# Output weights' low parts over the raw ones, the router's turned x in the queries' buffer, three buffers handed to expert weights earlier

## The chip, the cores and the metric

The kernel runs on one core of a Trainium2 chip. The metric is device time in microseconds (us) for one execution. All weights lie in the chip's main memory (DRAM) and are read during the run. The core's five engines run side by side: PE (matmuls), DVE and ACT (elementwise work, copies out of the accumulator memory), POOL (here small loads and a few elementwise operations) and SP, which in this kernel does nothing but issue transfers, in a fixed order, and wait for the semaphores ahead of each.

## The reference, cut to what matters

Two transformer blocks in float32 over 256 positions of width 1024. The first block ends in a mixture of 32 experts, of which each position uses two; the kernel reads the weights of all 32.

```python
y = concat([swa_sink_mixer(h_a), dilated_mixer(h_b), mla_mixer(h_c)]) @ w_out   # 1024 x 1024
x = layer_norm(ALPHA * x + y, ln1_g, ln1_b)
g_logits = x @ w_rg + b_rg                    # router: 4 groups, then 8 experts of the group
...
def block_ffn(xb, e):
    return (silu(xb @ w_gate[e]) * (xb @ w_up[e])) @ w_down[e]     # 3 MB of weights for each e
...
x = layer_norm(ALPHA * x + y_moe, ln2_g, ln2_b)
# then two layers: x = x + rms_norm(mixers(rms_norm(x) @ w_in[l]) @ w_out[l], post_norm[l])
```

## The kernel before

**Stages.** First the input products and the attention of the first block ("tile1" and "bv" jobs make queries, keys and values; steps A, C and B are the heads of its three mixers), then the output product ("y1"), layer norm and router ("logit", "rank"), then the experts, then the two layers of the second block.

**Split products.** The large products are made in three passes of a fast float format: a weight is split into a high part (ACT, line 1664, `high`) and a low part, weight minus high part (DVE, line 2336, `low`). The activations are split likewise into `a_high`, and `x_low` or `mix_low`. A split is a piece of weights for one product. The high parts lie in `w_high`, the low ones in `w_low`, each of six units of 4 KB per partition. `y1` has four splits, `w_out0` to `w_out3`, each of two units. Semaphore `lows` counts low parts done, `p_ready` counts products of PE done.

**Memory.** The buffer `ring` has 12 slots of 1 MB. The buffers of the split products lie over it: `w_high` is slots 5, 6, 7, `w_low` is slots 8, 9, 10, `a_high` is slot 11, `x_low` is the buffer `xT` and `mix_low` is `mixT` (the block at line 439 allocates them and frees them, so that `ring`, `xT` and `mixT` come to lie on the same addresses). Slots 0 to 4 take raw weights of the mixers in turn. After the last input product nothing reads `x_low`; ACT then writes the turned x for the router there (job `x1t`, line 1504), and PE reads it (line 1073).

**Expert weights.** Four experts form a bunch, so there are 8 bunches of 12 MB, each of 12 items of 1 MB: items 0 to 3 hold rows 0 to 511 of gate and up of the four experts, items 4 to 7 rows 512 to 1023, items 8 to 11 the down weights. Counted through, item n is item n mod 12 of bunch n div 12. On PE a bunch is `gate_up(b, 0)`, `gate_up(b, 1)` (line 1324), the gather of the rows of the next bunch (line 1280), `down(b)` (line 1339) and the sum into the output (line 1307). The semaphore `gu_half` is raised after the first, `gu_ready` after the second, `y_ready` twice in `down`.

**Who waits for what.** `load_expert` issues one item after `free_for_experts` has waited until its buffer is free. The first 21 items go to 21 buffers in the order of `FIRST_LOADS` (line 133): the 12 slots, and nine buffers of the attention stage that are free by then (`K_C`, `TILES_MID`, `BIAS_HIGH`, `BIAS_LOW`, `PROBS_T`, `V_TOP`, `MIX_T`, `LN_ROWS`, `X_T`). Four of them (`ONCE`) are used once, the other 17 in rotation: `expert_slots` (line 144) gives each later item the buffer that was given longest ago. The wait is then on the earlier item's product (`expert_done`: `gu_half` for items 0 to 3 of a bunch, `gu_ready` for 4 to 7, `y_ready` for 8 to 11). In the last bunch the rotation is broken: its items 0 to 3 must go to slots 0 to 3, which the next layers' weights take over (`NEXT_LAYERS`), and slots 9 to 11 are not used (`MORE_SLOTS`, kept for a second round of experts that these inputs do not need). SP issues strictly in program order, so an item whose buffer is not free holds all behind it.

In the kernel before, the bunch before the last has its items 0 to 11 in slots 3, 4, K_C, PROBS_T, V_TOP, 1, 2, 0, 6, 9, 7, 10.

Of the kernel before, what the change touches and what calls it, by code (L numbers as in the profile page):

```python
# [7 lines left out]
F32 = mybir.dt.float32  # L8
# [7 lines left out]
P = 128  # L16
# [107 lines left out]
for _l in range(LAYERS):  # L124
# [7 lines left out]
EARLY = ((0, 3), (1, 4))  # L132
FIRST_LOADS = EARLY + ((2, K_C), (16, TILES_MID), (17, BIAS_HIGH), (18, BIAS_LOW), (3, PROBS_T), (4, V_TOP), (5, 1),
                       (6, 2), (7, 0), (8, 6), (9, 9), (10, 7), (11, 10), (12, 5), (13, 8), (14, 11), (15, MIX_T),
                       (19, LN_ROWS), (20, X_T))
ONCE = (TILES_MID, BIAS_HIGH, BIAS_LOW, LN_ROWS)
# [24 lines left out]
MIXERS_RING = 5  # L161
TWICE_ROUND, LATE_RING = 2 * MIXERS_RING, 3
MEM_AT = 3
PIECES = {f"bunch{b}_{k}": 2 for b in range(BUNCHES) for k in range(GATE_UP)}


def slot_of(n):
    if n < FIRST_EXPERT:
        return n % MIXERS_RING if n < TWICE_ROUND else (n - TWICE_ROUND) % LATE_RING
    return EXPERT_SLOTS[n - FIRST_EXPERT] if n < FIRST2 else (n - FIRST2) % MIXERS_RING  # L170
# [217 lines left out]

LAST_SPLIT = {item_split(n): n for n in range(len(SPLITS))}
OPENING = [SPLIT[("tile1", 0)]] + [SPLIT[("tile2", l, 0)] for l in range(LAYERS)]  # L390
# [36 lines left out]
def build(nc, ins, out):  # L427
    ctx = ExitStack()
    with ctx:
# [8 lines left out]

        with nc.sbuf_tensor("slots_before", [P, MIXERS_RING * SLOT], F32), \
                nc.sbuf_tensor("w_high", [P, UNITS * SLOT // 2], F32R) as w_high, \  # L440
                nc.sbuf_tensor("w_low", [P, UNITS * SLOT // 2], F32R) as w_low, \
                nc.sbuf_tensor("a_high", [P, KC * T], F32R) as a_high, \
                nc.sbuf_tensor("x_low", [P, KC * T], F32R) as x_low, \
                nc.sbuf_tensor("mix_low", [P, KC * T], F32R) as mix_low:
            pass
# [33 lines left out]
        x4 = x_nat[:, :].rearrange("p (t k q) -> p t k q", t=2, k=KC)  # L479
        xT3 = xT[:, :].rearrange("p (k t) -> p k t", k=KC)  # L480
        y_nat = tiles[:, 0:2048].rearrange("p (t d) -> p t d", t=2)
        xT_1 = k_c[:, :].rearrange("p (k t) -> p k t", k=KC)
# [3 lines left out]
        def split_of(n):  # L486

            wide = P if SPLITS[n][0] in OF_TILES else COLS
            a = units_before(n) % UNITS * KC * P
            return [w[:, a:a + KC * wide].rearrange("p (k n) -> p k n", k=KC) for w in (w_high, w_low)]  # L490

# [195 lines left out]
        def _(sp):  # L687
# [53 lines left out]
            def free_for_experts(n):  # L741
# [3 lines left out]
                if earlier:  # L745
                    sp.wait_ge(*expert_done(earlier[-1]))
                elif k < MIXERS_RING:
                    used_up(max(m for m in range(FIRST_EXPERT) if slot_of(m) == k))
                elif k < RING - 1:
                    owners = {UNIT_OWNER[u] for u in range(units_before(OPENING[1])) if u % UNITS // 2 == (k - 5) % 3}  # L750
                    sp.wait_ge(p_ready, max(max(users(n)) for n in owners) + 1)
                elif k == K_C:
                    sp.wait_ge(scores, s_first(STEP[("C", 0, C_HEADS - 1)]) + 1)
                elif k == TILES_MID:
                    sp.wait_ge(scores, s_first(STEP[("B", 0, B_HEADS - 1)]) + 3)
                elif k in (BIAS_LOW, BIAS_HIGH):
                    sp.wait_ge(maxed, STEP[("B", 0, B_HEADS - 1)] + 1)
                elif k in (PROBS_T, V_TOP):
                    sp.wait_ge(o_ready, LAST_OUT_1)
                elif k == LN_ROWS:  # L760
                    sp.wait_ge(ln_done, 2)
                elif k == X_T:
                    sp.wait_ge(p_ready, JOB[("logit", 1)] + 1)
                else:
                    sp.wait_ge(p_ready, JOB[("y1", 3, 1)] + 1)
# [19 lines left out]
            for n in range(FIRST_EXPERT):  # L785
                if n >= MIXERS_RING:
                    used_up(max(m for m in range(n) if slot_of(m) == slot_of(n)))
# [11 lines left out]
                if n == 4:  # L799
                    sp.wait_ge(bias_out, 16)  # L800
                    sp.dma_start(bias3[:, 0:A_HEADS, :], shifted_rows(0, A_HEADS)).then_inc(bias_in, 16)
            for n in [i for i, _ in FIRST_LOADS[len(EARLY):]] + list(range(len(FIRST_LOADS), PER_BUNCH * (BUNCHES - 1))):
                load_expert(FIRST_EXPERT + n)
# [99 lines left out]
        def _(pe):  # L903
# [58 lines left out]
            def run(job, j):  # L962
# [104 lines left out]
                elif kind == "logit":  # L1067
                    tt = job[1]
                    pe.wait_ge(router_scaled, 1)
                    for k in range(KC):  # L1070
                        if k % 4 == 0:
                            from_act(("x1t", tt, k // 4))
                        mm = pe.matmul(dst[:, 0:GROUPS + EXPERTS], xT3[:, k, P * tt:P * tt + P], router[:, k, :],
                                       start=(k == 0), stop=(k == KC - 1))
# [402 lines left out]
        def _(act):  # L1477
# [13 lines left out]
            def take(job, j):  # L1491
# [10 lines left out]
                elif kind == "x1t":  # L1502
                    tt, half = job[1:]
                    op = act.activation(xT3[:, 4 * half:4 * half + 4, P * tt:P * tt + P],
                                        src.rearrange("p (c t) -> p c t", c=4), ACT.Copy)
# [1028 lines left out]
```

## Time and profile before

| | |
|---|---|
| median of 3 runs | 729.3 us (727.13 to 731.64) |
| the profiled execution, its own time | 730.15 us |
| its span | 728.2 us |
| mean granted clock of PE | 0.969 of full speed |
| busy: PE, DVE, ACT, POOL | 661.3, 353.1, 330.1, 43.8 us |
| moved by DMA | 167.84 MB, mean 230 GB/s |

The span is the profiled part of the execution; 1.95 us lie around it. The page cuts the span into 40 slices of 18.2 us and gives for each the busy tenths of each engine and the GB/s moved. Other views give instructions in order of time with the idle time ahead of each and what ended it, sums for chosen stretches, and the chain of work that ended last. A busy PE is not a PE at its peak: matmuls are pipelined and their ends are modelled.

### The profile page before, as it was taken

The page shows a single profiled execution, that of the slowest core. Times are in us where ns is not written, and L with a number is a line of the kernel's source. Part 1 is how long each engine was busy: PE and PEld are TensorE (multiplying, and loading weights), DVE is VectorE, ACT ScalarE, POOL GpSimd, SP SyncE. Part 2 cuts the span into 40 slices and gives each one's busy share as a digit, 9 for nine tenths or more (in the row PEclk, how much of TensorE's full clock was granted, in tenths as well). Part 3 has the DMA queues.
Part 4 walks back from the last instruction along what each step waited for, and adds up shares of the span by engine and source line. Part 5 has one row for each costly group of instructions (what it writes and reads, how often), then busy time and mean ns, then how long its engine had stood idle before and what let it go on. Part 6 is the DMA issues. An engine that isn't in the chain of part 4 may idle for free.

```text
span 728.2 us, 11783 instructions
## 1 busy us (share of the span) xinstructions
PE 661.3 (91%) x4605; PEld 513.0 (70%) x4606; DVE 353.1 (48%) x817; ACT 330.1 (45%) x776; POOL 43.8 (6%) x57
## 2 busy tenths in 40 slices
PE   6989999999899999789796999898979999889986
PEld 5967998789545436335262589877859899778876
DVE  1543656645531021011010557787765487877733
ACT  3465656541011122011120354778864647788642
POOL 6001000000000000000000322000000020100000
PEclk9999999999999999898898999999979999999999
DMA  9995327097999999999999857045533080171301
GB/s 275 338 298 173 118 86 232 23 333 280 363 410 412 412 415 409 415 411 411 416 391 409 268 167 237 1 129 162 161 130 116 15 276 1 57 234 60 114 1 59
DMA packets 94682, 167.84 MB, mean 230 GB/s; under 512 B 4271, under 2 KB 75713, under 8 KB 90529
## 3 DMA queue, kind: packets, MB, share of 16 engines
q1 hardware_dynamic: 92272, 160.88, 61.5%
q0 software_dynamic: 2224, 6.10, 2.5%
q8 instruction: 39, 0.64, 0.4%
q14 instruction: 19, 0.15, 0.1%
q10 hardware_dynamic: 128, 0.08, 0.0%
HBM read 165.96 MB, written 1.07 MB: 229 GB/s over the span
## 4 chain that ended last, share of the span: by engine, by line
PE 58%; SPq 13%; DMA 9%; DVE 8%; ACT 8%; issue 3%; DVEq 0%; ACTq 0%
SPq L777 11%; PE psum L909 11%; PE psum L911 10%; PE psum L910 10%; PE psum L1324 4%; PE psum L1280 3%; DMA values<-in_w_expert_down_dram 3%; PE psum L1214 2%; DMA ring<-in_w_expert_up_dram 2%; PE psum L1339 2%; PE psum L952 2%; PE psum L1044 2%; PE psum L1261 2%; SPq L780 2%; DMA ring<-in_w_in_dram 2%
## 5 line engine op out<-in xcount | busy, mean ns | idle before, releaser
L909 PE MATMUL psum<-a_high,w_high 128*128 128x256 f32 x512 | 150.1, 293 | 8.7 <-DVE w_low L2336 4.6
L911 PE MATMUL psum<-a_high,w_low 128*128 128x256 f32 x512 | 145.4, 284 | 0.0
L910 PE MATMUL psum<-x_low,w_high 128*128 128x256 f32 x512 | 145.3, 284 | 0.0
L2336 DVE TENSOR_TENSOR w_low<-ring,w_high 128x1024 fp32r<-128x1024 f32 (+1 forms) x76 | 107.7, 1429 | 17.4 <-ACT w_high L1664 17.4
L909 PEld LDWEIGHTS psum<-a_high,w_high 128*128 128x128 f32 x512 | 98.6, 193 | 18.5 <-issue 6.8
L1664 ACT ACTIVATE w_high<-ring 128x1024 fp32r<-128x1024 f32 (+1 forms) x79 | 96.1, 1220 | 14.1 <-DMA ring<-in_w_in_dram 10.8
L910 PEld LDWEIGHTS psum<-x_low,w_high 128*128 128x128 f32 x512 | 98.7, 193 | 0.1
L911 PEld LDWEIGHTS psum<-a_high,w_low 128*128 128x128 f32 x512 | 98.6, 193 | 0.0
L1324 PE MATMUL psum<-ring,q_c 128*32 128x512 f32 x336 | 64.6, 708 | 13.5 <-DMA ring<-in_w_expert_up_dram 8.0
L909 PE MATMUL psum<-w_high,a_high 128*128 128x256 f32 x240 | 69.9, 291 | 0.1
L910 PE MATMUL psum<-w_low,a_high 128*128 128x256 f32 x240 | 68.7, 286 | 0.0
L1280 PEld LDWEIGHTS psum<-tiles,x_nat 128*128 128x128 f32 x256 | 53.6, 299 | 7.5 <-issue 7.5
L2258 DVE TENSOR_TENSOR tiles<-tiles,psum 128x256 f32<-128x256 f32 x8 | 3.4, 421 | 110.3 <-ACT tiles L1714 110.2
L1280 PE MATMUL psum<-tiles,x_nat 128*128 128x128 f32 x256 | 55.1, 373 | 0.5 <-DVE tiles L2231 0.5
L911 PE MATMUL psum<-w_high,mix_low 128*128 128x256 f32 x192 | 55.0, 286 | 0.0
L909 PEld LDWEIGHTS psum<-w_high,a_high 128*128 128x128 f32 x240 | 46.9, 195 | 3.6 <-issue 2.3
L1712 ACT ACTIVATE tiles<-psum 128x256 f32<-128x256 f32 x8 | 3.1, 384 | 99.9 <-PE psum L1324 99.9
L1324 PEld LDWEIGHTS psum<-ring,q_c 128*32 128x32 f32 x336 | 16.2, 127 | 44.0 <-issue 44.0
L910 PEld LDWEIGHTS psum<-w_low,a_high 128*128 128x128 f32 x240 | 47.0, 196 | 0.0
L911 PEld LDWEIGHTS psum<-w_high,mix_low 128*128 128x128 f32 x192 | 37.7, 197 | 0.0
L1214 PE MATMUL psum<-const,probs 128*128 128x128 f32 x200 | 32.6, 285 | 4.1 <-ACT probsT L1634 3.0
L1634 ACT ACTIVATE probsT<-psum 128x512 f32<-128x512 f32 (+1 forms) x56 | 30.3, 547 | 9.5 <-PE psum L1214 8.6
(343 smaller groups left out, 1148.1 us busy)
## 6 DMA issues: line engine op xcount, KB each, us to landing
ring<-in_w_in_dram SPq DMA_DIRECT2D x36, 1024.0 KB, 9.1
ring<-in_w_expert_down_dram SPq DMA_DIRECT2D x22, 1024.0 KB, 17.7
ring<-in_w_expert_gate_dram SPq DMA_DIRECT2D x42, 512.0 KB, 14.8
ring<-in_w_expert_up_dram SPq DMA_DIRECT2D x42, 512.0 KB, 15.3
ring<-in_w_out_dram SPq DMA_DIRECT2D x12, 1024.0 KB, 5.0
ring<-in_w_mem_kv_dram SPq DMA_DIRECT2D x4, 1024.0 KB, 12.2
k_c<-in_w_expert_down_dram SPq DMA_DIRECT2D x3, 1024.0 KB, 17.4
probsT<-in_w_expert_gate_dram SPq DMA_DIRECT2D x4, 512.0 KB, 15.0
```

Of the source, the lines that this page charges most:

```text
L777: sp.dma_start(to[:, SLOT // 2 * m:SLOT // 2 * m + SLOT // 2].rearrange("p (k n) -> p k n", n=DE), w[:, 4 * half:4 * half + 4, :]).then_in ...
L780: sp.dma_start(to, ins["w_expert_down"][0, e].rearrange("(p k) n -> p (k n)", p=P)).then_inc(loaded[slot_of(n)], 16)
L909: pe.matmul(dst, left[0], right[0], start=first, stop=False)
L910: pe.matmul(dst, left[0], right[1], start=False, stop=False)
L911: return pe.matmul(dst, left[1], right[0], start=False, stop=last)
L952: mm = pe.matmul(dst, src[:, k, P * tt:P * tt + P], w[:, k, a:b], start=(k == 0), stop=(k == KC - 1))
L1214: mm = pe.transpose(dst[:, P * c:P * c + P], pr[:, a:a + P], ident)
L1280: mm = pe.matmul(dst[:, P * c:P * c + P], x[:, k, :], places2[:, tt, :], start=(tt == 0), stop=(tt == 1))
L1324: mm = pe.matmul(bank(6)[PLACES * e:PLACES * e + PLACES, :], gathered2[b % 2][:, k, PLACES * e:PLACES * e + PLACES], w, start=(k == 0), st ...
L1634: act.activation(probsT[:, 512 * (n % 4):512 * (n % 4) + w], bank(t_at(n))[:, 0:w], ACT.Copy).then_inc(turned_out, 1)
L1664: act.activation(split_like_raw(n)[0], raw_of(n), ACT.Copy).then_inc(highs, 1)
L2336: dve.tensor_tensor(w_l, raw_of(n), as_f32(w_h), ALU.subtract).then_inc(lows, 1)
```

## The change

Three things are changed, and no product, split or elementwise operation is added or removed.

1. The low part of each `y1` split is written over its own raw weights, in the slot where they were loaded (a new name, `slots_low`, stands for slots 0 to 4 in the split format). Its high part stays in `w_high`. `w_out3` is loaded into slot 8 and its low part stays there. So slots 9 and 10 hold nothing after the last input product (`LAST_INPUT`, the second half of `bv` of group 2). On the other hand a raw slot of `w_out` is now free only when its products are done, not when it is split (`LAST_SPLIT` leaves `y1` out).
2. The turned x for the router goes to `q_c`, where the queries of mixer C were, instead of `xT`. So `xT` too is free after the last input product.
3. `FIRST_LOADS` has a new order: items 3, 4 and 5 go to X_T, slot 9 and slot 10.

```diff
-FIRST_LOADS = EARLY + ((2, K_C), (16, TILES_MID), (17, BIAS_HIGH), (18, BIAS_LOW), (3, PROBS_T), (4, V_TOP), (5, 1),
-                       (6, 2), (7, 0), (8, 6), (9, 9), (10, 7), (11, 10), (12, 5), (13, 8), (14, 11), (15, MIX_T),
-                       (19, LN_ROWS), (20, X_T))
+FIRST_LOADS = EARLY + ((2, K_C), (3, X_T), (4, 9), (5, 10), (16, TILES_MID), (17, BIAS_HIGH), (18, BIAS_LOW),
+                       (6, PROBS_T), (7, V_TOP), (8, 0), (9, 1), (10, 6), (11, 2), (12, 7), (13, 5), (14, 8), (15, 11),
+                       (20, MIX_T), (19, LN_ROWS))
...
+    if n == LAST_OUT:
+        return LAST_OUT_SLOT
...
-LAST_SPLIT = {item_split(n): n for n in range(len(SPLITS))}
+LAST_INPUT = max(n for n, _job in enumerate(JOBS) if _job[0] in ("tile1", "bv"))
+LAST_SPLIT = {item_split(n): n for n in range(len(SPLITS)) if SPLITS[n][0] != "y1"}
...
+            if SPLITS[n][0] == "y1":
+                k = slot_of(item_split(n))
+                low = w_low[:, 0:SLOT] if k == LAST_OUT_SLOT else slots_low[:, SLOT * k:SLOT * k + SLOT]
...
-                elif k < MIXERS_RING:
+                elif k < MIXERS_RING or k == LAST_OUT_SLOT:
                     used_up(max(m for m in range(FIRST_EXPERT) if slot_of(m) == k))
+                elif k in (9, 10, X_T):
+                    sp.wait_ge(p_ready, LAST_INPUT + 1)
...
             for n in range(FIRST_EXPERT):
-                if n >= MIXERS_RING:
+                if n == LAST_OUT:
+                    for i in range(2, 4):
+                        load_expert(FIRST_EXPERT + i)
+                    sp.wait_ge(p_ready, LAST_INPUT + 1)
+                elif n >= MIXERS_RING:
                     used_up(max(m for m in range(n) if slot_of(m) == slot_of(n)))
...
-                        mm = pe.matmul(dst[:, 0:GROUPS + EXPERTS], xT3[:, k, P * tt:P * tt + P], router[:, k, :],
+                        mm = pe.matmul(dst[:, 0:GROUPS + EXPERTS], x1T[:, k, P * tt:P * tt + P], router[:, k, :],
...
-                    op = act.activation(xT3[:, 4 * half:4 * half + 4, P * tt:P * tt + P],
+                    op = act.activation(x1T[:, 4 * half:4 * half + 4, P * tt:P * tt + P],
```

**SP, from the last output weights on.** A row is one issue: the buffer written, the tensor read, the shape, and the semaphore waited for. Before:

```order
L720 DMA ring<-in_w_out_dram 128x8x256 [waits lows] x4
L777 DMA k_c<-in_w_expert_gate_dram 128x4x256 [waits scores]
L777 DMA k_c<-in_w_expert_up_dram 128x4x256
L777 DMA tiles<-in_w_expert_gate_dram 128x4x256 [waits scores]
L777 DMA tiles<-in_w_expert_up_dram 128x4x256
L777 DMA bias<-in_w_expert_gate_dram 128x4x256 [waits maxed]
L777 DMA bias<-in_w_expert_up_dram 128x4x256
L777 DMA bias<-in_w_expert_gate_dram 128x4x256 [waits maxed]
L777 DMA bias<-in_w_expert_up_dram 128x4x256
L777 DMA probsT<-in_w_expert_gate_dram 128x4x256 [waits o_ready]
```

After:

```order
L729 DMA ring<-in_w_out_dram 128x8x256 [waits lows] x3
L786 DMA k_c<-in_w_expert_gate_dram 128x4x256 [waits scores]
L786 DMA k_c<-in_w_expert_up_dram 128x4x256
L786 DMA xT<-in_w_expert_gate_dram 128x4x256 [waits p_ready]
L786 DMA xT<-in_w_expert_up_dram 128x4x256
L729 DMA ring<-in_w_out_dram 128x8x256 [waits p_ready]
L786 DMA ring<-in_w_expert_gate_dram 128x4x256 [waits p_ready]
L786 DMA ring<-in_w_expert_up_dram 128x4x256
L786 DMA ring<-in_w_expert_gate_dram 128x4x256 [waits p_ready]
L786 DMA ring<-in_w_expert_up_dram 128x4x256
L786 DMA tiles<-in_w_expert_gate_dram 128x4x256 [waits scores]
L786 DMA tiles<-in_w_expert_up_dram 128x4x256
```

The fourth output load and two pairs of expert loads for slots 9 and 10 now stand behind the pair for `xT`, all of them behind the wait on `p_ready` for the last input product, and ahead of the pairs for `tiles`, `bias` and `probsT`. Three items have moved ahead of the attention stage's own buffers.

**SP, at the start of the last bunch.** `gate` and `up` of one item make a pair. The first row is slot 0 (slots 1 and 2 read the same and are left out with the `up` rows), then come slots 3, 5, 8 and `mixT`; in the second list slots 3, 7, 5 and `mixT`. Before:

```order
L777 DMA ring<-in_w_expert_gate_dram 128x1024 [waits gu_ready]
L777 DMA ring<-in_w_expert_up_dram 128x1024
...
L777 DMA ring<-in_w_expert_gate_dram 128x1024 [waits gu_half]
...
L777 DMA ring<-in_w_expert_gate_dram 128x1024 [waits gu_ready]
...
L777 DMA ring<-in_w_expert_gate_dram 128x1024 [waits y_ready]
...
L777 DMA mixT<-in_w_expert_gate_dram 128x1024 [waits y_ready]
```

After:

```order
L786 DMA ring<-in_w_expert_gate_dram 128x1024 [waits y_ready]
L786 DMA ring<-in_w_expert_up_dram 128x1024
...
L786 DMA ring<-in_w_expert_gate_dram 128x1024 [waits gu_half]
...
L786 DMA ring<-in_w_expert_gate_dram 128x1024 [waits gu_ready]
...
L786 DMA ring<-in_w_expert_gate_dram 128x1024 [waits y_ready]
...
L786 DMA mixT<-in_w_expert_gate_dram 128x1024 [waits y_ready]
```

What moved is the semaphore ahead of the first three pairs, `gu_ready` before and `y_ready` after: in the changed kernel slots 0, 1 and 2 hold items 8, 9 and 11 of the bunch before the last, down weights, where they held items 7, 5 and 6. The rotation gives that bunch the slots 3, 4, K_C, X_T, 9, 10, PROBS_T, V_TOP, 0, 1, 6, 2. On PE, DVE, ACT and POOL the order of instructions is unchanged; only the buffers that they name differ.

## Rows read from the trace of the kernel before

**Rows 1.** The page, part 2: GB/s moved in 40 slices of 18.2 us

```profile
GB/s 275 338 298 173 118 86 232 23 333 280 363 410 412 412 415 409 415 411 411 416 391 409 268 167 237 1 129 162 161 130 116 15 276 1 57 234 60 114 1 59
```

**Rows 2.** Stretches: engines' busy us, then granted clock, DMA share, GB/s

```profile
130.00:140.00 10.00, 8.76 (x60) 6.57 (x59) 6.58 (x17) 5.80 (x14) 0.00 (x0) 1.00 0.00 1
...
192.00:194.00 2.00, 1.92 (x20) 0.81 (x24) 0.00 (x0) 0.00 (x0) 0.00 (x0) 1.00 1.11 349
200.00:250.00 50.00, 47.17 (x311) 23.52 (x303) 8.54 (x32) 7.06 (x16) 1.79 (x3) 1.00 1.02 412
```

**Rows 3.** SP in order of time: start, us, line, buffer and tensor, count

```profile
142.99 0.37 SPq L777 DMA_DIRECT2D tiles<-in_w_expert_gate_dram  x1
...
172.95 5.81 SPq L780 DMA_DIRECT2D ring<-in_w_expert_down_dram  x4
...
194.59 1.42 SPq L780 DMA_DIRECT2D xT<-in_w_expert_down_dram  x1
196.05 0.91 SPq L780 DMA_DIRECT2D ring<-in_w_expert_down_dram  x2
```

**Rows 4.** ACT in order of time, at the end of the last input product

```profile
131.58 0.38 ACT L1538 ACTIVATE values<-psum 128x256 f32<-128x256 f32 x1 [0.38 <-PE psum L911]
...
158.62 1.92 ACT L1664 ACTIVATE w_high<-ring 128x2048 fp32r<-128x2048 f32 x1 [3.33 <-PE psum L911]
```

**Rows 5.** DVE in order of time: takings of `y1` products (L1959), a low part (L2336)

```profile
158.56 0.42 DVE L1959 SCALAR_TENSOR_TENSOR x_nat<-x_nat,psum 128x256 f32<-128x256 f32 x1 [0.26 <-PE psum L911]
...
161.78 2.28 DVE L2336 TENSOR_TENSOR w_low<-ring,w_high 128x2048 fp32r<-128x2048 f32 x1
164.32 0.42 DVE L1959 SCALAR_TENSOR_TENSOR x_nat<-x_nat,psum 128x256 f32<-128x256 f32 x1 [0.26 <-PE psum L911]
```

**Rows 6.** Chain of work that ended last: start, us, what

```profile
192.08 3.64 PE psum L1324 x32
...
380.36 21.86 DMA values<-in_w_expert_down_dram
402.35 3.67 PE psum L1339 x32
```

**Rows 7.** Stretches of 2 us where transfers restart after a pause

```profile
172.00:174.00 2.00, 1.92 (x16) 1.54 (x14) 0.63 (x3) 1.09 (x3) 0.00 (x0) 1.00 0.24 29
174.00:176.00 2.00, 1.92 (x15) 1.64 (x15) 1.83 (x3) 1.20 (x2) 0.00 (x0) 1.00 0.82 274
```

**Rows 8.** PE in order of time, last two bunches: start, us, instruction, idle before

```profile
359.17 1.03 PE L1324 MATMUL psum<-values,q_c 128*32 128x512 f32 x1 [3.41 <-DMA ring<-in_w_expert_up_dram]
365.67 7.88 PE L1280 MATMUL psum<-tiles,x_nat 128*128 128x128 f32 x32
374.52 3.64 PE L1339 MATMUL psum<-ring,tiles 128*32 128x512 f32 x32 [0.51 <-ACT tiles L1719]
379.06 3.67 PE L1307 MATMUL psum<-values,tiles 128*128 128x512 f32 x8 [0.32 <-DVE values L2264]
387.51 6.48 PE L1324 MATMUL psum<-ring,q_c 128*32 128x512 f32 x34 [4.78 <-issue]
396.93 1.99 PE L1271 MATMUL psum<-const 128*128 128x256 f32 x8
...
400.29 1.56 PE L1271 MATMUL psum<-const 128*128 128x256 f32 x6 [0.47 <-ACT tiles L1719]
```

**Rows 9.** SP in order of time, from bunch 6's down weights on

```profile
343.68 6.26 SPq L780 DMA_DIRECT2D ring<-in_w_expert_down_dram  x4
365.80 0.33 SPq L777 DMA_DIRECT2D ring<-in_w_expert_gate_dram  x1
```

**Rows 10.** Waits of SP from 340 to 400 us: total us, times, longest

```profile
SPq L777 <- PE psum L1324: 14.9, 1, 14.9
```

**Rows 11.** Stretches of 2 us around the last bunch's first issue

```profile
358.00:360.00 2.00, 0.83 (x5) 0.24 (x9) 0.00 (x0) 0.00 (x0) 0.00 (x0) 0.57 1.02 420
...
368.00:370.00 2.00, 2.00 (x10) 2.00 (x10) 0.00 (x0) 0.22 (x1) 0.00 (x0) 1.00 0.98 342
```

More of the change, by code:

```diff
@@ L162 @@
 TWICE_ROUND, LATE_RING = 2 * MIXERS_RING, 3
+LAST_OUT, LAST_OUT_SLOT = ITEM["w_out3"], 8
 MEM_AT = 3
@@ L434, in sem @@
             return ctx.enter_context(nc.semaphore(name))
-        with nc.sbuf_tensor("slots_before", [P, MIXERS_RING * SLOT], F32), \
+        with nc.sbuf_tensor("slots_low", [P, MIXERS_RING * SLOT], F32R) as slots_low, \
                 nc.sbuf_tensor("w_high", [P, UNITS * SLOT // 2], F32R) as w_high, \
@@ L480, in build @@
         xT3 = xT[:, :].rearrange("p (k t) -> p k t", k=KC)
+        x1T = q_c[:, :].rearrange("p (k t) -> p k t", k=KC)
         y_nat = tiles[:, 0:2048].rearrange("p (t d) -> p t d", t=2)
@@ L489, in split_of @@
             a = units_before(n) % UNITS * KC * P
-            return [w[:, a:a + KC * wide].rearrange("p (k n) -> p k n", k=KC) for w in (w_high, w_low)]
+            high, low = w_high[:, a:a + KC * wide], w_low[:, a:a + KC * wide]
+            if SPLITS[n][0] == "y1":
+                k = slot_of(item_split(n))
+                low = w_low[:, 0:SLOT] if k == LAST_OUT_SLOT else slots_low[:, SLOT * k:SLOT * k + SLOT]
+            return [w.rearrange("p (k n) -> p k n", k=KC) for w in (high, low)]
         def raw_of(n):
@@ L746, in free_for_experts @@
                     sp.wait_ge(*expert_done(earlier[-1]))
-                elif k < MIXERS_RING:
+                elif k < MIXERS_RING or k == LAST_OUT_SLOT:
                     used_up(max(m for m in range(FIRST_EXPERT) if slot_of(m) == k))
-                elif k < RING - 1:
-                    owners = {UNIT_OWNER[u] for u in range(units_before(OPENING[1])) if u % UNITS // 2 == (k - 5) % 3}
+                elif k in (9, 10, X_T):
+                    sp.wait_ge(p_ready, LAST_INPUT + 1)
+                elif k < 8:
+                    owners = {UNIT_OWNER[u] for u in range(units_before(OPENING[1])) if u % UNITS // 2 == k - 5}
                     sp.wait_ge(p_ready, max(max(users(n)) for n in owners) + 1)
@@ L761, in free_for_experts @@
                     sp.wait_ge(ln_done, 2)
-                elif k == X_T:
-                    sp.wait_ge(p_ready, JOB[("logit", 1)] + 1)
                 else:
@@ L801, in _ @@
                     sp.dma_start(bias3[:, 0:A_HEADS, :], shifted_rows(0, A_HEADS)).then_inc(bias_in, 16)
-            for n in [i for i, _ in FIRST_LOADS[len(EARLY):]] + list(range(len(FIRST_LOADS), PER_BUNCH * (BUNCHES - 1))):
+            for n in [i for i, _ in FIRST_LOADS[len(EARLY) + 2:]] + list(range(len(FIRST_LOADS), PER_BUNCH * (BUNCHES - 1))):
                 load_expert(FIRST_EXPERT + n)
```

## The prediction

> **What bounds the kernel now.** First I read the GB/s line of the page [rows 1]: in slices 12 to 22, from 200 to 400 us, it stands at 391 to 416, while in slices 4 to 8 it falls to 23 in one. So the experts are bound by the stream of their weights, and there is idle transfer time ahead of them. The stretches say it closer: 412 GB/s from 200 to 250 us, 1 GB/s from 130 to 140 us, and 349 GB/s where items of bunches 0 and 1 are moved, whose gate and up weights go in rows of 1 KB [rows 2]. A MB (1.049 million bytes) takes 2.55 us at 412 and 3.0 us at 349. A bunch of 12 MB takes 30.5 us; on PE it takes 3.6 + 3.6 + 7.9 + 3.6 + 3.7 us and small gaps, 24 us in all (each kind has its row in [rows 6, 8]). PE waits for the second half's weights in bunch 6, for 3.41 us [rows 8], and the last thing waited for is the last down weight, at 402.35 us [rows 6]. What is loaded before the experts begin is worth its stream time, as long as the stream then never stops. So I had to look for two things: how many MB more are loaded ahead, and where the stream might stop.
>
> **Loaded ahead: 2 MB, not 3.** The last input product is done at 131.6 us, when ACT takes it [rows 4]. From there the changed SP issues X_T, `w_out3`, and slots 9 and 10: 4 MB of 1 KB rows, 12 us, into a stretch in which nothing is moved [rows 2]. They are through by 145 us; the pairs for `tiles` and `bias`, issued at 142.99 us in before [rows 3], follow at most 2 us late and are needed first at 220 us. `w_out3` comes some 19 us before ACT makes its high part at 158.62 us [rows 4]. Then slots 0 and 1 are no longer free at their split but at their products, 158.6 and 164.3 us [rows 5]; and they now take down weights. Slot 6 and slot 2 wait for the seventh of the eight `y1` products, which is at 172.95 us, the point where before issues slots 6 and 9 [rows 3]. So at 173 us 13 items of the first 21 are in, where it was 11; the same 2 MB are issued there, and from the last product on (178 us) 6 MB are left, where it was 8: five at 3.0 and one at 2.55 us (before, five and three). With the 2 MB of 173 us through at 174.5 + 5.1 = 179.6 (the start is worked out below), the 21st item is in at 202.2 us before and 197.2 us after. The 22nd waits for bunch 0's first half: 192.08 + 3.64 us [rows 6], and SP then issues, at 195.9 us at best (before, it issued at 196.05, behind its backlog [rows 3]).
>
> **A restart costs 1.6 us.** At 172.95 us the queue was empty [rows 3]. The two stretches that follow moved 29 and 274 GB/s [rows 7], (29 + 274) x 2 / 412 = 1.47 us of full rate, so full rate began in effect at 174.5, 1.6 us after the issue. The bounds are 0 (a queue that still holds work) and 3 us (no byte until 176). The Trainium skill, "DMA: Bandwidth & Descriptors", section "Latency and other measured facts", gives 0.6 us to the first byte for transfers issued from SP; by that figure each restart would cost 1.0 us less and the time below would be 1 us shorter. The trace's 1.6 is for this kernel's pattern, and I take that.
>
> So the stream resumes at 195.9 + 1.6 = 197.5 us, and the gain that goes into bunch 1 is g = 202.2 - 197.5 = 4.7 us. Does it survive? I walked the waits on: after 21 items, 4 MB are released at 196, 4 at 202, 4 at 214 (`y_ready` of bunch 0), 4 at 222, 4 at 238. The stream needs 10.2 us for each four and 5.1 us more for the memory and norm rows that POOL loads at 226, so it holds work at each of these points, by 5 us at the tightest (238 us: 243.3 against 237.9). From bunch 4 on PE waits for the stream, and everything is 4.7 us earlier.
>
> **The new wait: the last bunch.** Its items 0 to 3 must go to slots 0 to 3. Before, slots 0, 1 and 2 held items 7, 5 and 6 of bunch 6 and were free at `gu_ready`; now they hold its items 8, 9 and 11 and are free at `y_ready`, behind the second half of `down`. SP issues in order, so all 12 MB of the last bunch, and behind them the next layers' weights, are held. In before this wait was 14.9 us long already [rows 10] and ended at 365.80 us [rows 9], 0.13 us after gate and up of bunch 6 (365.67, where the next row of PE begins [rows 8]). It cost little, because the four down items issued at 343.68 us were still moving: the stream fell only to 342 GB/s at 368 to 370 us and recovered [rows 11]. Now the issue comes after gather, turn and `down`: 374.52 + 3.64 - 365.67 = 12.5 us later on PE's own clock [rows 8]. Everything issued before has landed by then and there is nothing else to move; slots 7, 5, 8 and MIX_T are free, but stand behind in the order.
>
> **The sum.** After: 365.67 - 4.7 = 361.0 gate and up of bunch 6 done; + 12.5 `y_ready`, 373.5; + 1.6 restart; + 30.5 for 12 MB; + 1.0 until PE sees the last one (between 0 and 2.4: rates alone put the last byte of before 1.4 us ahead of PE's start at 402.35), 406.6 us. Before: 402.35 [rows 6]. That is +4.2 us for the stream; as a formula, 8.9 - g.
>
> PE may add to it. In before PE idled for 4.78 us ahead of the last bunch and its first half then took 6.1 us, not 3.6; so too after 3.41 us in bunch 6, 6.5 us [rows 8]. The granted clock there was 0.57 of full speed in one stretch that begins in the idle time [rows 11]: the lower level, 1.2 GHz, for most of such a half. In the changed kernel the first 4 MB are in at 373.5 + 1.6 + 10.2 + 1.0 = 386.3, PE having idled since 379.06 + 3.67 - 4.7 = 378.0; first half until 392.6. The next four are in at 396.4: 3.8 us of idling again, so I take the second half at 6.4 us too, to 402.8. From there to being ready for `down` PE needs 400.29 + 1.56 - 396.93 = 4.9 us [rows 8]: 407.7, +5.4 us. The bounds are the stream's +4.2 and, with the first half also late, +7. I take +5.2. Behind `down` all is a chain of PE, DVE and ACT with the next weights queued behind the same stream, so it passes through whole.
>
> **What costs nothing.** The low parts move to other addresses with the same shape; one takes 2.28 us [rows 5] on the same engine in the same place. The same holds for the turned x. If writing over the operand being read were slower, by as much as its own length, `w_out2` and `w_out3` would each have 2.3 us more; each has a product pair of 5.8 us between (158.56 to 164.32 [rows 5]), which covers it.
>
> The profiled execution took 730.15 us (span 728.2), 0.85 above the median of 729.3. 730.15 + 5.2 = 735.4, and against the median 734.5 us.
>
> **Rivals.**
> 1. The gain arrives and the new wait costs nothing: 729.3 - 4.7 = 724.6 us. It decides by whether the stream still holds 12.5 + 1.6 us of work at `gu_ready` of bunch 6, 5.5 MB. There are four down items issued behind the second half's, 10.2 us at most, and the stream dips at 368 us in before [rows 11]. Against it: every row here. For it: the intent to load early does reach the stream. 10%.
> 2. The two cancel: 727 to 731.5. If a smaller idle time spares PE the low clock in bunch 6, its second half takes 3.6 in place of 6.5 us and `y_ready` comes 2.9 us earlier; with the last bunch at full clock the sum is 8.9 - 4.7 - 2.9 = +1.3 us, 730.6. What speaks against: the idle time is set by stream and PE pace, both as before. 22%.
> 3. The gain is lost early: the 22nd item's restart leaves the 16 DMA engines ragged, or the 4 MB at 131 us shift the attention stage. g = 1 gives 7.9 + 1.2 for the low clock, +9.1, 738.4 us. For it: 197.2 against 195.9 is close. Against: 1 us of gap is already in. 16%.
> **Chances.** Forecast (732.5 to 737) 52%, rivals 10, 22 and 16%. A change of 1%, 7.3 us, is about what a measurement of this kernel can tell from none. Faster than 722.0: only rival 1 with some help, 4%. Slower than 736.6: rival 3 and the upper end of the forecast, 26%. Within: 70%. The range leaves out rival 1 and the far end of rival 3: 728.5 to 739.5 us.
>
> **What would show it.** In the changed profile: issues to `xT` and the ring at 131.6 to 136 us; the last of the first 21 items issued some 5 us earlier; a wait of SP's expert loads on the `down` product (L1339 before) ahead of the last bunch, ending near 373.5 us; a pause of 5 to 10 us in the GB/s between 365 and 376 us, where none was; the last down weight at 406 to 408 us. If there is no pause, rival 1 holds and I have miscounted what was issued. If the pause is there and the time is no longer, bunch 6 was faster than I let it be (its second half shorter than 5 us). If the time is over 738, the stream before 250 us shows a second gap.

## The result, and the profile after

| | before | after |
|---|---|---|
| median | 730.5 us (727.1 to 733.0, 6 runs) | 738.4 us (734.3 to 742.4, 6 runs) |
| ratio to before, 95% interval | | 1.0136 (1.0097 to 1.0175) |
| the profiled execution, its span | 730.15, 728.2 us | 740.1, 738.2 us |

The changed kernel is slower by 1.4% (0.97 to 1.75%, that is 7 to 13 us), where I forecast 5.2 us. The two medians are 7.9 us apart, the two profiled executions 10.0 us. Work on the engines is what it was: the page of after begins with the same busy times to 1 us. What differs is the line of the GB/s moved in each slice of 18.5 us, which answers to [rows 1]:

```profile
span 738.2 us, 11783 instructions
...
PE 660.7 (89%) x4605; PEld 512.8 (69%) x4606; DVE 352.3 (48%) x817; ACT 330.4 (45%) x776; POOL 43.8 (6%) x57
...
GB/s 273 340 287 184 124 65 173 270 304 249 378 387 417 408 415 412 412 417 408 308 209 417 342 103 291 9 72 214 82 204 115 1 265 22 11 275 58 115 1 58
```

Slice 8 (129 to 148 us) has 270 where before had 23: the early loads are there. Slices 20 and 21 (351 to 388 us) have 308 and 209 where the stream of before went on at about 400: a hole at the start of the last bunch.

The order of time on SP, which only issues, shows both places. The columns are start, length, line and what is written and read; they answer to [rows 3, 9].

```profile
131.88 0.37 SPq L786 DMA_DIRECT2D xT<-in_w_expert_gate_dram  x1
...
132.84 0.51 SPq L729 DMA_DIRECT2D ring<-in_w_out_dram  x1
...
138.18 1.33 SPq L786 DMA_DIRECT2D ring<-in_w_expert_up_dram  x1
143.30 0.37 SPq L786 DMA_DIRECT2D tiles<-in_w_expert_gate_dram  x1
...
188.84 0.37 SPq L786 DMA_DIRECT2D tiles<-in_w_expert_gate_dram  x1
...
196.08 0.82 SPq L789 DMA_DIRECT2D ring<-in_w_expert_down_dram  x2
...
375.08 0.33 SPq L786 DMA_DIRECT2D ring<-in_w_expert_gate_dram  x1
```

The four items are issued at 131.9 to 139.5 us (131.6 to 136 was forecast), the last of the first 21 items goes out at 188.84 instead of 194.59 us, and the 22nd waits for bunch 0's first half, to 196.08. The last bunch is issued at 375.08, in before at 365.80 [rows 9].

PE in the last two bunches, in order of time (answers to [rows 8]; in brackets the idle time ahead of a row and what ended it):

```profile
356.17 1.07 PE L1337 MATMUL psum<-ring,q_c 128*32 128x512 f32 x2 [3.57 <-DMA values<-in_w_expert_up_dram]
...
362.53 7.88 PE L1293 MATMUL psum<-tiles,x_nat 128*128 128x128 f32 x32
371.38 3.64 PE L1352 MATMUL psum<-ring,tiles 128*32 128x512 f32 x32 [0.51 <-ACT tiles L1732]
...
390.59 6.29 PE L1337 MATMUL psum<-ring,q_c 128*32 128x512 f32 x32 [10.99 <-DMA ring<-in_w_expert_up_dram]
...
400.82 1.08 PE L1337 MATMUL psum<-ring,q_c 128*32 128x512 f32 x3 [3.94 <-DMA mixT<-in_w_expert_up_dram]
...
407.04 1.99 PE L1284 MATMUL psum<-const 128*128 128x256 f32 x8
...
411.89 0.62 PE L1352 MATMUL psum<-ring,tiles 128*32 128x512 f32 x1
```

Gate and up of bunch 6 are done 3.1 us earlier than in before (362.53 against 365.67: this row, the gather, begins as they end). The last `down` begins at 411.9 us, against 402.35: 9.6 us later. From gather to last `down` it was 36.7 us and is 49.4. What lies behind the last `down` takes nearly the same, 326.3 us against 325.9. So 9.6 of the 10.0 us are here, and the attention stage has next to no part in it: bunch 0 begins at 192.39 against 192.08 us.

The stretches around the pause (length, busy PE, PEld, DVE, ACT, POOL, then granted clock, DMA share, GB/s):

```profile
364.00:366.00 2.00, 2.00 (x10) 2.00 (x10) 0.82 (x2) 0.00 (x0) 0.00 (x0) 1.00 0.29 123
366.00:368.00 2.00, 2.00 (x10) 2.00 (x10) 0.00 (x0) 0.60 (x1) 0.00 (x0) 1.00 0.00 0
...
376.00:378.00 2.00, 2.00 (x5) 0.95 (x6) 0.00 (x0) 1.21 (x4) 0.00 (x0) 1.00 0.83 244
378.00:380.00 2.00, 1.59 (x4) 0.38 (x2) 0.00 (x0) 0.00 (x0) 0.00 (x0) 1.00 0.90 229
380.00:382.00 2.00, 0.00 (x0) 0.00 (x0) 0.00 (x0) 0.00 (x0) 0.00 (x0) 1.00 0.98 375
...
384.00:386.00 2.00, 0.00 (x0) 0.00 (x0) 0.00 (x0) 0.00 (x0) 0.00 (x0) 0.50 0.99 342
```

The stream stands still from 365 to 376 us, moves little over half its rate for 4 us more, and PE, idle, is at the lower clock level (0.50 of full speed, 1.2 GHz) when its weights come.

### The profile page after: what moved, and what is told of

It reads as the page before. It is cut to its first block, busy times and chain, and to the rows that moved or that the text cites. A ratio compares the mean times of both kernels' runs of the same rounds, so it can differ in the third digit from the quotient of the medians.

```text
span 738.2 us, 11783 instructions
## 1 busy us (share of the span) xinstructions
PE 660.7 (89%) x4605; PEld 512.8 (69%) x4606; DVE 352.3 (48%) x817; ACT 330.4 (45%) x776; POOL 43.8 (6%) x57
## 4 chain that ended last, share of the span: by engine, by line
PE 60%; SPq 12%; DVE 9%; DMA 8%; ACT 8%; issue 3%; DVEq 0%; ACTq 0%
PE psum L922 10%; SPq L786 10%; PE psum L923 10%; PE psum L924 10%; PE psum L1337 5%; PE psum L1293 4%; PE psum L1352 2%; PE psum L1227 2%; DMA values<-in_w_expert_up_dram 2%; DMA mixT<-in_w_expert_up_dram 2%; PE psum L965 2%; PE psum L1057 2%; DMA ring<-in_w_in_dram 2%; PE psum L1274 2%; DVE w_low L2349 2%
## 5 line engine op out<-in xcount | busy, mean ns | idle before, releaser
L2349 DVE TENSOR_TENSOR w_low<-ring,w_high 128x1024 fp32r<-128x1024 f32 (+1 forms) x73 | 100.9, 1394 | 17.9 <-ACT w_high L1677 17.9
L1677 ACT ACTIVATE w_high<-ring 128x1024 fp32r<-128x1024 f32 (+1 forms) x79 | 96.1, 1220 | 13.6 <-DMA ring<-in_w_in_dram 10.3
L923 PE MATMUL psum<-w_low,a_high 128*128 128x256 f32 x192 | 54.8, 285 | 0.0
L923 PEld LDWEIGHTS psum<-w_low,a_high 128*128 128x128 f32 x192 | 37.4, 195 | 0.0
```

Source lines behind the costliest of these rows:

```text
L923: pe.matmul(dst, left[0], right[1], start=False, stop=False)
L1677: act.activation(split_like_raw(n)[0], raw_of(n), ACT.Copy).then_inc(highs, 1)
L2349: dve.tensor_tensor(w_l, raw_of(n), as_f32(w_h), ALU.subtract).then_inc(lows, 1)
```

## The experiments

Theory W: the loss is the wait of the last bunch on `y_ready`, which came in because the new `FIRST_LOADS` gives slots 0, 1 and 2 to down items. Rival R: something else of the change costs it (the low parts over the raw ones, the moved x, the early loads' traffic), and the wait is incidental. All edits are small; the ratios are to the kernel before on the same chip. Since executions of one kernel lie up to 10 us apart, I also give for each profile the two stretches that the argument is about, read as above:

| profile | bunch 0's first half done to gather of bunch 6 | gather of bunch 6 to last `down` |
|---|---|---|
| before | 169.9 us | 36.7 us |
| after | 166.5 | 49.4 |
| e1, wait undone | 164.6 | 36.9 |
| e9, the same again | 165.3 | 37.5 |
| e8, one MB more | 164.8 | 36.7 |
| e2, wait alone | 169.7 | 49.2 |
| e3, free items first | 162.9 | 41.8 |
| e6, e1 and e3 | 165.6 | 39.4 |
| e5, down items first | 165.1 | 58.5 |
| e4, one MB early | 166.3 | 38.2 |

The first column is the gain of the early loads, the second the price of the last bunch. After, e3 and e5 are the same program up to the last bunch and yet have 166.5, 162.9 and 165.1 us, so a difference of up to 4 us in the first column does not tell two kernels apart. All seven profiles with the full early loads lie below the 169.9 and 169.7 us of before and e2.

### e1_gu_wait: the changed kernel without the wait

Only the item numbers in the order of loading change; every buffer is loaded at the same place. Bunch 6 then has its items 5, 6 and 7 in slots 0, 1 and 2.

```diff
-FIRST_LOADS = EARLY + ((2, K_C), (3, X_T), (4, 9), (5, 10), (16, TILES_MID), (17, BIAS_HIGH), (18, BIAS_LOW),
-                       (6, PROBS_T), (7, V_TOP), (8, 0), (9, 1), (10, 6), (11, 2), (12, 7), ...
+FIRST_LOADS = EARLY + ((2, K_C), (3, X_T), (8, 9), (9, 10), (16, TILES_MID), (17, BIAS_HIGH), (18, BIAS_LOW),
+                       (10, PROBS_T), (4, V_TOP), (5, 0), (6, 1), (11, 6), (7, 2), (12, 7), ...
```

> The changed kernel with the same loads at the same points, but other item numbers: slots 9, 10, PROBS_T and 6 take down items 8 to 11 of bunch 0, and V_TOP, 0, 1, 2 its items 4 to 7, so that in bunch 6 slots 0, 1, 2 are free at gu_ready again. Theory W (the wait on y_ready ahead of the last bunch is the whole loss, and some 3 us of the gain reach bunch 6, as the changed profile has it): 730.5 - 3 = 727.5 us, a ratio of 0.996 to before, and no pause of the stream at 366 to 375 us. Rival R (the early loads, or the low parts over raw slots, cost the time, for instance by disturbing the stream at 200 us): it stays near the changed kernel's 738.4, ratio 1.011.

Measured: 723.3 us (721.4 to 729.5, 10 runs), ratio 0.9923 (0.9883 to 0.9963). That is a larger gain than theory W's 0.996; the interval just reaches it. The last bunch is issued 0.13 us after gate and up of bunch 6, and there is no pause. SP's row and the stretches of this kernel:

```profile
363.15 0.33 SPq L786 DMA_DIRECT2D ring<-in_w_expert_gate_dram  x1
```

```profile
362.00:380.00 18.00, 17.18 (x92) 11.08 (x84) 1.96 (x4) 4.85 (x11) 0.00 (x0) 1.00 1.02 410
```

410 GB/s over the 18 us in which after has its hole. The low parts, the moved x and the four early items are all still in, so R falls: with the wait gone, nothing of the loss is left, and the early loads do gain. In the table the stretch from gather to last `down` is 12.5 us shorter than in after. The edit also changes which kinds of items go early (slots 9 and 10 and PROBS_T take down items); e2 below has the wait without that.

### e9_gu_wait_again: the same kernel on another chip

No edit against e1.

> The same kernel as e1_gu_wait, timed again beside the next three so that they can be compared on one chip. 0.992 of before, 724 us.

Measured: 727.0 us (721.8 to 729.5, 12 runs), ratio 0.9944 (0.9911 to 0.9977). The two intervals overlap from 0.9911 to 0.9963; the gain, 4 to 6 us by the ratios, is clear of none in both.

### e2_wait_alone: the kernel before with the wait put in

No load is issued earlier and no buffer is used differently; slots 1, 2 and 0 get items 8, 9 and 10.

```diff
-... (3, PROBS_T), (4, V_TOP), (5, 1), (6, 2), (7, 0), (8, 6), (9, 9), (10, 7), (11, 10), (12, 5), ...
+... (3, PROBS_T), (4, V_TOP), (8, 1), (9, 2), (10, 0), (5, 6), (6, 9), (7, 7), (11, 10), (12, 5), ...
```

> The kernel before, with nothing loaded earlier and no buffer changed; only item numbers are exchanged, so that in bunch 6 slots 1, 2, 0 hold items 8, 9, 10 and the last bunch waits on y_ready. Theory W: before plus what the wait costs by the changed profile, 9.6 us of shift at the last down plus the 3.0 us that it was ahead at bunch 6, 12.6 in all: 743 us, ratio 1.017. Rival R: 730.5, ratio 1.000. My prediction's own size for it was 8.9 + 1.2 = 10.1: 740.6.

Measured: 743.6 us (740.7 to 749.7, 4 runs), ratio 1.0185 (1.0117 to 1.0253), so some 13.6 us, with an interval of 5 us to each side. The view of waits (semaphore's releaser, sum, times, longest) and two rows of PE:

```profile
SPq L777 <- PE psum L1339: 43.1, 4, 27.1
```

```profile
372.18 7.89 PE L1280 MATMUL psum<-tiles,x_nat 128*128 128x128 f32 x32
...
399.94 6.41 PE L1324 MATMUL psum<-ring,q_c 128*32 128x512 f32 x32 [10.71 <-DMA ring<-in_w_expert_up_dram]
```

SP stands for 27.1 us on the `down` product, where it stood for 14.9 on gate and up in before [rows 10]: 12.2 us longer. PE's idle time (10.71 us against 10.99) and the 49.2 us from gather to last `down` (49.4) are those of after, without any other part of the change. This execution, 749.65 us, is longer than the wait explains, by about 7 us: its bunch 0 begins at 196.93 us, 4.8 us late, behind a stretch at low granted clock from 140 us on, and its first half takes 5.5 us. That belongs to the execution, and the medians are the fairer measure.

### e3_free_first: the changed kernel, waiting items issued last

Items 4 to 7 of the last bunch have buffers that are free at `gu_half` and `gu_ready` or were free before; they are issued ahead of items 0 to 3, which still wait.

```diff
-            for n in range(FIRST2 - PER_BUNCH, FIRST2):
-                load_expert(n)
+            for j in (4, 5, 6, 7, 0, 1, 2, 3, 8, 9, 10, 11):
+                load_expert(FIRST2 - PER_BUNCH + j)
```

> The changed kernel, with items 4 to 7 of the last bunch issued ahead of its items 0 to 3: their buffers 7, 5, 8 and MIX_T are free long before. Theory W: 4 MB move in the pause, the stream restarts only for 8 MB at 375 us, the last down is in at about 397 to 399 us and PE, not the stream, is last: 727 to 731 us, ratio 0.996 to 1.000. Rival R: 738, as the changed kernel.

Measured: 732.1 us (728.2 to 736.6, 10 runs), ratio 1.0046 (1.0009 to 1.0083). It wins some 6 us of the 10 back, and misses the expected range. The stretches show why the stream is no longer at fault, and the row of PE what is:

```profile
362.00:376.00 14.00, 13.17 (x73) 9.38 (x74) 1.96 (x4) 4.05 (x9) 0.00 (x0) 1.00 1.01 409
```

```profile
388.90 6.08 PE L1337 MATMUL psum<-ring,q_c 128*32 128x512 f32 x35 [10.82 <-DMA ring<-in_w_expert_up_dram]
```

The hole is filled, at 409 GB/s. But PE needs items 0 to 3 first, gets them no earlier than in after (388.9 against 390.6), idles as long, and runs its first half at the low clock. After that it waits for no transfer: PE is now what ends last. Order of issue must follow order of use as well as freedom of buffers.

### e5_down_first: where the slow start sits

The wait on `y_ready` is kept for the whole last bunch, and its four down items go first. Theory P said that the low rate after the restart goes with the gate and up items (rows of 4 KB at a distance of 8 KB), theory S that it goes with the restart.

```diff
-            for n in range(FIRST2 - PER_BUNCH, FIRST2):
-                load_expert(n)
+            sp.wait_ge(y_ready, 2 * (BUNCHES - 1))
+            for j in (8, 9, 10, 11, 0, 1, 2, 3, 4, 5, 6, 7):
+                load_expert(FIRST2 - PER_BUNCH + j)
```

> The changed kernel, where after the same wait on y_ready the last bunch's four down items (1 MB in one piece, rows of 8 KB) are issued first, then its gate and up items. One look at the restart. Theory P (the slow first microseconds after a restart, 244 and 229 GB/s in the changed profile, come from the pattern of the gate and up items): the first 4 us after the restart move at 400 or more, and the slow stretch comes later, with the gate and up items. Theory S (every restart is slow, whatever is issued): 230 to 250 GB/s again at 2 to 4 us behind the issue. The time itself: items 0 to 3 come 10.2 us later and PE works behind the stream, 744 to 747 us.

One execution, 746.3 us, within the 744 to 747 expected. The issue is at 375.85 us, and the stretches are:

```profile
376.00:378.00 2.00, 1.68 (x7) 0.81 (x6) 0.54 (x1) 1.57 (x4) 0.00 (x0) 1.00 0.55 135
378.00:380.00 2.00, 2.00 (x6) 0.76 (x4) 0.00 (x0) 0.00 (x0) 0.00 (x0) 1.00 0.98 410
...
386.00:388.00 2.00, 0.00 (x0) 0.00 (x0) 0.00 (x0) 0.00 (x0) 0.00 (x0) 0.50 0.97 406
388.00:390.00 2.00, 0.00 (x0) 0.00 (x0) 0.00 (x0) 0.00 (x0) 0.00 (x0) 0.50 1.06 305
390.00:392.00 2.00, 0.00 (x0) 0.00 (x0) 0.00 (x0) 0.00 (x0) 0.00 (x0) 0.50 0.97 322
392.00:394.00 2.00, 0.00 (x0) 0.00 (x0) 0.00 (x0) 0.00 (x0) 0.00 (x0) 0.50 1.02 418
```

Down items are at full rate 2 us after the issue: (0.15 us of nothing before 376, then 135 of 412) makes 1.5 us, the 1.6 that I had read in before. The slow stretch comes 12 us later, when the four down items (10.2 us) are through and the gate and up items begin. P holds in this run: it is not the restart by itself that is slow. Nor is it the kind of item by itself, since e1 moves gate and up items at 410 GB/s; both have to come together (see the last section). This rests on one execution.

### e8_one_more: is the gain capped?

On e1, one item (13, for slot 5) is issued behind the fourth of the eight `y1` products (165.5 us) instead of after the last one (178.2 us). Theory F said that with all buffers full by bunch 0's first half, another MB is worth nothing; L said that it is worth its 2.5 us.

```diff
-... (5, 0), (6, 1), (11, 6), (7, 2), (12, 7), (13, 5), (14, 8), ...
+... (5, 0), (6, 1), (13, 5), (11, 6), (7, 2), (12, 7), (14, 8), ...
```

> e1_gu_wait with one more MB ahead: item 13 goes to slot 5 behind slot 1, at the fourth y1 product (164.3 us), where the stream is idle until 173 us. Theory F (all 21 buffers are full by then, so the 22nd item waits for bunch 0's first half at 196 us and the gain is capped at the 4.7 us between 197.5 and 202.2): the same as e1_gu_wait, 0.992 of before, with a longer pause of the stream at 194 to 198 us. Rival L (each MB ahead is worth its 2.5 us): 0.9885 of before.

Measured: 723.6 us (720.3 to 728.6, 12 runs), ratio 0.9929 (0.9896 to 0.9962); e9, on the same chip, had 0.9944. The stretches of this kernel:

```profile
166.00:172.00 6.00, 6.00 (x52) 6.00 (x51) 2.08 (x4) 0.00 (x0) 0.00 (x0) 1.00 1.00 334
...
194.00:196.00 2.00, 2.00 (x24) 0.63 (x16) 0.00 (x0) 0.00 (x0) 0.00 (x0) 1.00 0.47 150
196.00:198.00 2.00, 2.00 (x18) 1.65 (x15) 0.00 (x0) 0.00 (x0) 0.00 (x0) 1.00 0.32 39
```

The MB does move early: 334 GB/s at 166 to 172 us, where e9 has 175. It is then paid back as a pause at 194 to 198 us, until SP can issue the 22nd item at 196.48. The first column of the table is unchanged (164.8). The trace speaks for F. The times by themselves do not decide: L's 0.9885 lies below the interval, but a MB's 2.5 us counted from e9's 0.9944 would be 0.991, which lies in it. From the end of bunch 0's first half to the start of bunch 6's second half e8 has 159.7 us, where e1 and e9 have 159.6 and 160.4: the MB is not seen there.

### e4_xt_only: one MB earlier, no new wait

In the kernel before, the turned x goes to the queries' buffer and X_T is loaded early, with item 3. The low parts stay where they were, and the last bunch waits on `gu_ready`.

```diff
-                       (3, PROBS_T), (4, V_TOP), (5, 1), (6, 2), (7, 0), (8, 6), (9, 9), (10, 7), ...
+FIRST_LOADS = EARLY + ((2, K_C), (3, X_T), (16, TILES_MID), ..., (8, PROBS_T), (4, V_TOP), (5, 1), (6, 2), (7, 0), ...
...
+        x1T = q_c[:, :].rearrange("p (k t) -> p k t", k=KC)
...
-                    sp.wait_ge(p_ready, JOB[("logit", 1)] + 1)
+                    sp.wait_ge(p_ready, LAST_INPUT + 1)
```

> The kernel before with one part of the change alone: the router's turned x in q_c and an expert item in X_T right after the last input product. The low parts of y1 stay in w_low and slots 9 and 10 load as before; item numbers are chosen so that the last bunch still waits on gu_ready. By my count the whole change has 2 MB more in at 173 us and this one has 1 MB: 2.5 to 3 us less than before, ratio 0.996. If the three buffers counted for a MB each it would be the same 2.5 us here and 7.6 in the whole; if earlier loads are worth nothing, 1.000.

Measured: 728.4 us (726.6 to 731.3, 12 runs), ratio 0.9978 (0.9952 to 1.0004). That agrees with a MB's 2.5 to 3 us, and the interval still touches none; the time is inconclusive by itself. The trace says more. From the end of bunch 0's first half to the start of bunch 6's second half it was 163.4 us in before, 161.0 here and 160.1 in after: the stream gained 2.4 us with one MB and 3.3 with two.

### e6_both: e1 with the free items first

> e1_gu_wait with items 4 to 7 of the last bunch issued first. In e1 the stream had no pause around 365 us (408 to 418 GB/s from 362 to 380 us), so nothing is left to fill there; PE gets items 0 to 3 10 us later and has to do both halves behind them, but is ready before the down weights if its clock is back. 0.992 of before, the same as e1, if the stream bounds the end; up to 2 us more if PE does.

The edit is that of e3 on e1. Measured: 729.9 us (728.0 to 732.1, 12 runs), ratio 1.0014 (0.9986 to 1.0042), where I expected 0.992 to 0.995: a miss. Items 0 to 3 now come behind four others, and PE pays:

```profile
389.43 6.02 PE L1337 MATMUL psum<-ring,q_c 128*32 128x512 f32 x35 [8.58 <-DMA ring<-in_w_expert_up_dram]
```

In e1 this row starts at 384.88 us, and the last `down` waits 1.42 us for its weights; here it waits for none and starts at 403.24, against 399.89. Together with e3: the order 4 to 7 first costs by delaying PE, with or without the hole.

## Why the prediction failed

The mechanism stood: early loads gain a few us, and the last bunch's new wait costs more. Direction and places were right. The size was not: I took +5.2 us for the shift of the last `down` and it was 9.6 in the profile. Two terms were mis-sized: the way from the last bunch's issue to PE's start, taken as 12.8 us, measured 15.5 (the restart and the landing, +2.7), and the gain of the early loads, taken as 4.7 us, measured 3.1 (+1.6). The forecast of 734.5 us, with "within 1%" as the likeliest, met 738.4, of which 1.2 us is that before's median of 6 runs is 730.5 where that of 3 was 729.3. The number 738.4 is also that of my third rival, but by another road: its g was 1, the trace has 3.1.

**Loaded ahead: 2 MB, not 3.** Right. Issues at 131.9 us, the 21st item issued 5.75 us earlier, the 22nd at 196.08 (195.9 at best was said). e8's trace shows that it is the full buffers that cap the gain, and e2 that without early loads there is none (169.7 against 169.9 us in the first column).

**The gain g = 4.7.** Too large in every run with the early loads, by 1.2 us on the mean. The stream's own gain is read ahead of bunch 6's second half, which waits for its weights; behind it PE's clock mixes in. From the end of bunch 0's first half to there it was 163.4 us in before and e2, and 3.1 to 4.1 us less in after, e1, e3, e5, e6, e8 and e9, 3.5 on the mean. After, with 3.3, is one of them and no outlier. The larger gains of up to 7.0 us in the first column of the table come from the second half itself: at the low clock throughout it takes 6.5 us in before and 6.4 in after, where the clock comes back early it takes 5.0 in e1, and in e3, at full clock, 3.6. These are its starts; the gather, which begins as it ends, is at 363.02 and 361.01 us:

```profile
357.98 1.03 PE L1337 MATMUL psum<-values,q_c 128*32 128x512 f32 x1 [4.91 <-DMA ring<-in_w_expert_up_dram]
```

```profile
357.44 0.62 PE L1337 MATMUL psum<-ring,q_c 128*32 128x512 f32 x2 [3.98 <-DMA values<-in_w_expert_up_dram]
```

This is what my second rival named, the low clock spared in bunch 6. It does happen, in some executions, and not because the idle time is shorter: 3.98 us in e3, 3.41 in before. After has the low clock through nearly all of it.

After's stretches show a loss that the sum did not have (before had 347, 348, 426 and 403 in these four):

```profile
194.00:196.00 2.00, 2.00 (x21) 0.51 (x13) 0.00 (x0) 0.00 (x0) 0.00 (x0) 1.00 1.00 356
196.00:198.00 2.00, 2.00 (x21) 1.99 (x18) 0.00 (x0) 0.00 (x0) 0.00 (x0) 1.00 1.08 325
...
206.00:208.00 2.00, 2.00 (x20) 2.00 (x20) 0.00 (x0) 0.21 (x1) 0.00 (x0) 1.00 0.99 281
208.00:210.00 2.00, 2.00 (x18) 1.81 (x17) 0.20 (x1) 0.81 (x2) 0.00 (x0) 1.00 0.92 309
```

At 206 to 210 us (131 + 103) x 2 / 412 = 1.1 us are lost. All seven profiles with the early loads have such a dip, worth 0.7 to 1.1 us, and before, e2 and e4 have none. 4.7 - 1.1 = 3.6 fits the 3.5 us measured; that the dip is all of the difference is an estimate.

**The new wait, +12.5 us.** Right to 0.1 us: the gather begins at 362.53, the issue is at 375.08, 12.55 us later, and 12.55 in e2 too. "It cost little in before" was right as well: e1 has no hole, and from gather to last `down` it has 36.9 us against 36.7. But the stream of before did not fall "only to 342"; the next 2 us were lower still, and that is the slow start of gate and up items on a small scale:

```profile
370.00:372.00 2.00, 2.00 (x10) 2.00 (x10) 0.00 (x0) 0.38 (x1) 0.00 (x0) 1.00 0.97 315
```

**A restart costs 1.6 us.** This is the step that failed most. From the issue to PE's start on the first 4 MB I had 1.6 + 10.2 + 1.0 = 12.8 us; it was 390.59 - 375.08 = 15.5 in after and 399.94 - 384.73 = 15.2 in e2. Added up over the stretches, the 4 MB had been moved by about 388.4 us, so the restart took 388.4 - 375.1 - 10.2 = 3.1 us of full rate, and from there to PE's start 2.2 (I had taken 1.0 between 0 and 2.4). The same sums give 2.9 and 2.1 in e2. I had read the 1.6 from down items [rows 7], and e5 gives the same for them; the last bunch begins with gate and up items, which start at 244 and 229 GB/s. The quarters of a us around 376 show when the first bytes came:

```profile
375.75:376.00 0.25, 0.08 (x1) 0.11 (x1) 0.03 (x1) 0.25 (x1) 0.00 (x0) 1.00 0.00 0
376.00:376.25 0.25, 0.25 (x1) 0.19 (x2) 0.00 (x0) 0.25 (x2) 0.00 (x0) 1.00 0.68 131
```

So 0.9 us of the 3.1 pass before the trace records a byte, and the other 2.2 are lost to the low rate behind it. The Trainium skill, "DMA: Bandwidth & Descriptors", section "Latency and other measured facts", has 0.6 us to the first byte; by that figure the sum would have been a further 1.0 us off. The traces have 0.9 to 1.2 us in after, 0.8 to 1.0 in e2 and 0.9 to 1.1 in before at 173 us, and either way the first byte is not the price of a restart.

My bounds for the restart, 0 and 3, nearly held it, and the landing lay within its own. The bounds of +4.2 to +7 us that I gave for the shift did not add up both upper ends, 5.2 + 1.4 + 1.4 = 8.0; the range for the whole, up to 739.5 us, was wide enough for 738.4.

**The sum.** Everything behind is a shift: issue 375.1 instead of 373.5 (the missing 1.6 of g), then 2.7 us for restart and landing. Both halves of the last bunch did run at the low clock, 6.3 and 6.2 us (6.3 and 6.4 taken), with the second one 3.9 us late (3.8 said), and from there to the last `down` it was 4.8 us (4.9 said). PE's own way, which I had at +5.4 us, decides: 5.4 + 1.6 + 2.7 = 9.7, and 9.6 was measured. One reading was off without effect: the first half of the last bunch in before took 5.9 us, not 6.1, as the second begins at 393.40. My sign for a time over 738 us was a second gap of the stream before 250 us; the dip at 206 us is there, but the larger part of the miss lies at the last bunch.

**What costs nothing.** Right. A low part written over its raw weights takes what it took elsewhere, 2.28 us as in [rows 5]. The line of after on which the low parts into the raw slots are made (count, shortest, median and longest in ns, when):

```profile
L2349 DVE TENSOR_TENSOR slots_low<-ring,w_high x3: 2286/2286/2286, 117.7 to 156.3; 128x2048 fp32r<-128x2048 f32 x3
```

**The chances.** 26% for slower by over 1% was too low. The sum had two unknowns at the same place (restart and landing), both taken near the middle of their bounds, and both came out near or over the upper end.

## What to carry to other kernels

When buffers rotate, the place of an item in the list of first loads decides what holds each buffer at the end of the run; look at the last use of every buffer, not only at the first. A queue that issues in order turns one late buffer into a stop for all behind it, so give the first items after a hand-over to buffers that come free earliest among those needed first (e1: 0.6 to 0.8% faster than before and 11 to 15 us faster than the changed kernel, with only item numbers exchanged). And do not expect to gain from loading ahead beyond the point at which all buffers are full: in e8 the extra MB came back as a pause.

## What the hardware did that I had not expected

Gate and up items, whose rows of 4 KB lie 8 KB apart, are slow for about 4 us when they are the first of their kind after the stream has run low or dry, at 229 to 322 GB/s in the last bunch with the DMA engines 0.83 to 1.06 busy: at 376 to 380 us in after (244, 229), 386 to 390 in e2 (272, 250), 388 to 392 in e5 (305, 322). A milder dip stands at 368 to 372 us in before (342, 315), where the queue had run low. The same dip stands at 206 to 210 us in after (281, 309), 208 to 212 in e1 (317, 305) and 206 to 210 in e8 (328, 303), some 10 us after bunch 0's first half released the 22nd item to a queue that had run low or dry. Before and e4, which still had items queued at 196 us, have over 400 there. In the steady stream the same change of kind, once in every bunch, shows no dip: from 212 to 360 us no stretch of 2 us in before or after is below 390. Why is open; no run here tells it.

The other is that executions of one kernel differ by spells at low granted clock whose place changes. Before's profile has 0.83 in the stretch 520 to 550 us, where e8's has 1.00, and e2's has 0.66 at 140 to 150 us. The two rows, before and then e8:

```profile
520.00:550.00 30.00, 26.08 (x176) 20.73 (x175) 19.58 (x38) 18.82 (x43) 0.00 (x0) 0.83 0.44 141
```

```profile
520.00:550.00 30.00, 24.97 (x201) 22.05 (x201) 20.26 (x35) 19.64 (x47) 0.00 (x0) 1.00 0.48 156
```

A single profile is thus good to a few us for the whole, while a short stretch between two events can be good to some tenths, as the 49.4 and 49.2 us from gather to last `down` in after and e2 show. Over a long one it is not: the first column of the table spreads by 3.6 us over after, e3 and e5, which run the same program there.
